# The order of work inside the chunk steps of a two-stack transformer kernel

## The chip, the cores and the metric

The kernel runs on one NeuronCore of a Trainium2 chip, in one launch. The metric is the device time of that core in microseconds (us). The engines are TensorE (PE, with its weight loads as PEld), VectorE (DVE), ScalarE (ACT), GpSimd (POOL) and SyncE (SP). All arithmetic is in float32.

## What is computed

The reference runs two stacks of two layers over a sequence of 512 rows of width 1024. Only the first stack is touched here. In it each layer holds a hybrid mixer (pooling, differential attention and a bidirectional RWKV-7 scan) and an MLP. The two parts that meet in the changed code are the attention and the scan, cut to what matters:

```python
def block(args):                       # attention, one block of 128 queries
    logits = jnp.einsum('bqhmd,bkhmd->bhmqk', q_blk, k) + bias
    p = jax.nn.softmax(logits, axis=-1)
    attn = p[:, :, 0] - lam * p[:, :, 1]
    return jnp.einsum('bhqk,bkhd->bqhd', attn, v)

def step(state, inp):                  # scan, per head, forwards and backwards
    sa = jnp.einsum('bhij,bhj->bhi', state, -kk_t)
    state = state * w_t + sa[..., None] * (kk_t * a_t) + v_t[..., None] * k_t
    return state, jnp.einsum('bhij,bhj->bhi', state, r_t)
```

## The kernel before, in words

The first stack has two layers, and each layer has four channel groups, so `group_pe`, `group_act` and `group_dve` run eight times. A group computes one attention head (two softmax maps `m`), and two RWKV heads in both directions `d`. After projections and the inversion of a triangular matrix per chunk (`level_w` to `corner_t`), the group goes through the **chunk steps**, the loop `for s in range(NCH)` at L892 with four steps of 128 rows. This text calls the four steps of one group a stage; there are eight stages in an execution. Every engine has its own program, and its order is written out by hand.

TensorE in a step, in the order of before:

- R products: per direction two 64-column products per head (L897), and from step 1 on the product with the state (L904), which waits for VectorE's state of the step before.
- The attention's value products of the block before (`heads_out(s - 1)`, L858, four products of 128x128 accumulated), from step 1 on.
- The attention's logits of the next block (`logits(s + 1)`, L851, two products of 64 rows by 512 columns), except in the last step.
- U products (L914), which need ScalarE's copies of R.
- State and output products (L923, L926, L928), then those that need ScalarE's copies of U (L932, L936).
- Four transposes of the block's probabilities (`turn`, L2096), after a wait for VectorE's `pnorm(s)`.

After the last step `heads_out(3)` follows. Each float32 product is recorded as two matmul instructions, so L897 counts x8 in a step; a transpose is one.

ScalarE copies PSUM tiles to SBUF in the order in which `gA` lists them (`take`, L958): R of both directions, the attention output `o`, U of both directions, the transposed probabilities `PT`. Then `probs(s + 1)` (L985) takes the two exponentials of the next block. VectorE does `pnorm(s)` (L1155 to L1160), `rowmax(s + 1)` (L1147, one reduction per map, out of the logits' PSUM tile), the state from the S tiles (L1221 to L1231), and the Y tiles (L1237, L1239).

PSUM tiles rotate through banks in the order of the two lists `gA` (banks 0 and 1, taken by ScalarE) and `gV` (banks 2 to 7, taken by VectorE). A tile can be opened once the tile two places (for `gA`) or six places (for `gV`) ahead in the list has been taken. R's two tiles are opened together, so R of the next step waits until ScalarE has copied the transposed probabilities. Within a step the U products wait for the copy of R of their direction (`took`, L911). No DMA is issued inside the steps.

Of the kernel before, what the change touches and what calls it, by code (L numbers as in the profile page):

```python
# [23 lines left out]
P = 128  # L24
D = 1024
S = 512
# [9 lines left out]
NCH = S // CHUNK  # L36
# [199 lines left out]
def build(nc, x_in, wts1, const1, onehot, rel_bias, meta, wts2, const2, out):  # L236
    ctx = ExitStack()
    with ctx:
# [337 lines left out]
        gV += [f"W{d}{h}_{HB}" for d in range(2) for h in range(2)] + ["l00", "l01"]  # L576
        gV += [f"T{d}{h}_{HB}" for d in range(2) for h in range(2)]
        for s in range(NCH):
            gA += [f"R{d}{s}" for d in range(2)] + [f"o{s - 1}"] * (s > 0) + [f"U{d}{s}" for d in range(2)] + [f"PT{s}"]
            if s < NCH - 1:  # L580
                gV += [f"l{s + 1}{m}" for m in range(2)] + [f"S{d}{s}" for d in range(2)]
            gV += [f"Y{d}{s}" for d in range(2)]
        gA += [f"o{NCH - 1}"]
        gA += ["yt", "oT"]
        grpA, grpV = Tiles(gA, BA), Tiles(gV, BV)
# [150 lines left out]
        def group_pe(pe, L, c, proj, proj_rows, slot, free, flush, turn, meet):  # L736
# [155 lines left out]
            for s in range(NCH):  # L892
                o = a.open_all([f"R{d}{s}" for d in range(2)])
                for d in range(2):
                    n = chunk[d][s]
                    for h in range(2):
                        m = pe.matmul(o[d][:, 64 * h:64 * h + 64], g2[d][h][:, n, 0, :], vN[:, n, 64 * h:64 * h + 64],  # L897
                                      start=h == 0, stop=s == 0, skip_group_check=True)
                    if s == 0:
                        a.close(m)  # L900
                if s:
                    for d in range(2):
                        took(pe, grpV, vb, v_taken, f"S{d}{s - 1}")
                        a.close(pe.matmul(o[d][:, 0:P], ar[d][:, chunk[d][s], 0, :], state[d], start=False, stop=True,  # L904
                                          skip_group_check=True))
                    heads_out(s - 1)
                if s < NCH - 1:
                    logits(s + 1)
                for d in range(2):
                    n = chunk[d][s]  # L910
                    took(pe, grpA, ab, a_taken, f"R{d}{s}")  # L911
                    o = a.open(f"U{d}{s}")
                    for h in range(2):
                        m = pe.matmul(o[:, 64 * h:64 * h + 64], TT[d][h][:, n, :], Rs[d][:, 64 * h:64 * h + 64],  # L914
                                      start=h == 0, stop=True, skip_group_check=True)
                    a.close(m)
                last = s == NCH - 1
                o = v.open_all([f"S{d}{s}" for d in range(2) if not last] + [f"Y{d}{s}" for d in range(2)])
                so, yo = o[:-2], o[-2:]
                for d in range(2):  # L920
                    n = chunk[d][s]
                    if not last:
                        pe.matmul(so[d][:, 0:P], kN[d][:, n, :], vN[:, n, :], start=True, stop=False, skip_group_check=True)  # L923
                    for h in range(2):
                        c_ = slice(64 * h, 64 * h + 64)
                        pe.matmul(yo[d][:, c_], g2[d][h][:, n, 1, :], vN[:, n, c_], start=h == 0, stop=False, skip_group_check=True)  # L926
                    if s:
                        pe.matmul(yo[d][:, 0:P], ar[d][:, n, 1, :], state[d], start=False, stop=False, skip_group_check=True)  # L928
                for d in range(2):
                    took(pe, grpA, ab, a_taken, f"U{d}{s}")  # L930
                    if not last:
                        v.close(pe.matmul(so[d][:, 0:P], bN[d][:, chunk[d][s], :], Us[d], start=False, stop=True, skip_group_check=True))  # L932
                for d in range(2):
                    for h in range(2):
                        c_ = slice(64 * h, 64 * h + 64)
                        m = pe.matmul(yo[d][:, c_], g1[d][h][:, chunk[d][s], 1, :], Us[d][:, c_], start=False, stop=True, skip_group_check=True)  # L936
                    v.close(m)
                pe.wait_ge(*at("pnorm", it, s))
                turn(a, f"PT{s}", [pr[s % 2][:, 0, b * P:(b + 1) * P] for b in range(4)])
            heads_out(NCH - 1)  # L940
# [7 lines left out]
        def group_act(act, L, c, meet):  # L948
            it = L * GROUPS + c
            ab, vb = a_grp(L, c), v_grp(L, c)  # L950
            a = Taker(act, grpA, ab, a_made, a_taken)

            def col(name):
                return gp[:, GC[name]:GC[name] + 1]

            def take(name, dst, f=ACT.Copy, n=S, **kw):
                o = a.open(name)
                a.close(act.activation(dst, o[:, 0:n], f, **kw))  # L958

            def flat(z):  # L960
                return z.rearrange("p a b -> p (a b)")

            act.dma_start(skew, skew_dram[bass.ds(c, 1), P - 1:P - 1 + P * (LINE - 1)]
                          .rearrange("o (p n) -> (o p) n", n=LINE - 1)[:, 0:SKEW]).then_inc(skew_loaded, 16)
            for i, n in enumerate(("zr", "zk", "zv")):
                take(n, zp[:, i, 1:S + 1])
            act.wait_ge(*at("params", it))
            for t, buf in (("w", sig), ("a", aa)):
                for d in range(2):
                    take(f"{t}{d}", buf[:, d, :], ACT.Sigmoid, bias=col(f"{t}0_{d}"))  # L970
            take("u", up_[:, 8:8 + S])
            act.wait_ge(*at("ssq_max", it))
            act.activation(sq, kk, ACT.Sqrt).then_inc(STEPS["nrm_root"][0], 1)

            def exps(d):
                act.wait_ge(*at("cums", it, d))
                act.activation(ep[d][:, 0, :], cumx[d], ACT.Exp, scale=-KAPPA)
                act.activation(ep[d][:, 1, :], cum[d], ACT.Exp, scale=-KAPPA)
                act.activation(en[d], cum[d], ACT.Exp, scale=KAPPA)
                act.activation(e0[:, d, :], mid[:, d, :], ACT.Exp, scale=-KAPPA).then_inc(STEPS["exps"][0], 1)  # L980

            def probs(i):
                for m in range(2):
                    act.wait_ge(*at("logit_max", it, 2 * i + m))
                    act.activation(pr[i % 2][:, m, :], pr[i % 2][:, m, :], ACT.Exp, scale=-1.0, bias=ast[:, 16 * (i % 2) + m:16 * (i % 2) + m + 1],  # L985
                                   accum_out=ast[:, 16 * (i % 2) + 2 + m:16 * (i % 2) + 3 + m]).then_inc(STEPS["probs"][0], 1)

            take("aq", aq, scale=64 ** -0.5)
            take("ak", ak)
            exps(0)  # L990
            take("av", flat(av))
            exps(1)
            take("gate", gate)
            take("vN", flat(vN))
            for d in range(2):
                take(f"bN{d}", flat(bN[d]))
                take(f"kN{d}", flat(kN[d]))
            o = a.open("pool")
            a.close(act.activation(flat(yT[:, bass.ds(c, 1), :]), o, ACT.Copy, scale=col("pscale")))
            probs(0)  # L1000
            for s in range(NCH):
                for d in range(2):
                    take(f"R{d}{s}", Rs[d], n=P)
                if s:
                    take(f"o{s - 1}", osb[:, s - 1, :], n=P)
                for d in range(2):
                    take(f"U{d}{s}", Us[d], n=P)
                take(f"PT{s}", flat(pT))
                if s < NCH - 1:
                    probs(s + 1)  # L1010
            take(f"o{NCH - 1}", osb[:, NCH - 1, :], n=P)
            act.wait_ge(*at("osub", it))
            act.activation(ast[:, 12:16], ast[:, 8:12], ACT.Sqrt).then_inc(STEPS["osqrt"][0], 1)
            act.wait_ge(*at("gn_var", it))
            act.activation(gns[:, 2, :], gns[:, 1, :], ACT.Sqrt).then_inc(STEPS["gn_root"][0], 1)
            take("yt", kt[0], ACT.Identity, scale=col("gng"), bias=col("gnb"))

            act.wait_ge(*at("onorm", it))
            take("oT", flat(yT[:, bass.ds(c + 4, 1), :]), scale=ast[:, 7:8])
            a.end()  # L1020
            meet(m_grp(L, c, 0))
# [9 lines left out]
        def group_dve(dve, L, c, meet):  # L1031
# [182 lines left out]
            for s in range(NCH):  # L1214
                pnorm(s)
                if s < NCH - 1:
                    rowmax(s + 1)
                    if s:
                        for d in range(2):
                            n = chunk[d][s]  # L1220
# [12 lines left out]
                for d in range(2):  # L1233
                    n = chunk[d][s]
                    o = v.open(f"Y{d}{s}")
                    if s < 2:
                        v.close(dve.tensor_copy(ysum[:, n, :], o[:, 0:P]))  # L1237
                    else:
                        v.close(tt(ysum[:, n, :], ysum[:, n, :], o[:, 0:P], ALU.add))  # L1239
                dve.drain()  # L1240

            took(dve, grpA, ab, a_taken, "o3")
# [1375 lines left out]
```

## Time and profile before

| | us |
|---|---|
| time, median of 3 runs | 4862.07 (4854.64 to 4862.35) |
| time of the profiled execution | 4859.53 |
| its span in the profile | 4857.8 |
| TensorE busy | 4502.2 (93% of the span) |
| VectorE busy | 1481.6 (30%) |
| ScalarE busy | 828.7 (17%) |
| mean granted TensorE clock | 0.953 of full speed |

The span is the time from the first to the last instruction that the profile shows; the execution's own time is 1.7 us longer. The granted clock is a share of 2.4 GHz: 1.00 is 2.4 GHz and 0.50 is 1.2 GHz. Matmul records are modelled at their ends, so the start times of the groups are what counts: the distance from the start of one group to the start of the next is what the group costs.

### The profile page before, as it was taken

Reading aid. Unit: us, or ns where it says so; the run is one execution under the profiler, and the core shown is the slowest. Engines: PE = TensorE matmul, PEld = TensorE weight load, DVE = VectorE, ACT = ScalarE, POOL = GpSimd, SP = SyncE. Lnnn points to the kernel's source line nnn. Section 1 sums busy time; section 2 is a strip of 40 time slices with the busy share of each in tenths; the row PEclk is TensorE's granted clock in tenths of the full one; section 3 lists DMA queues with packets and bytes.
Section 4 is the critical chain, followed back from the end, with each engine's and each line's share of the span. In section 5 each row is a group of like instructions: output and inputs, shape, how many; then the busy total and the mean of one; then the engine's idle time right before and its main releaser. Section 6 shows DMA issues by size and latency. Waiting matters only on the chain.

```text
span 4857.8 us, 60662 instructions
## 1 busy us (share of the span) xinstructions
PE 4502.2 (93%) x25140; PEld 2959.1 (61%) x25140; DVE 1481.6 (30%) x3621; ACT 828.7 (17%) x2097; POOL 146.4 (3%) x144
## 2 busy tenths in 40 slices
PE   7888898998999888888998999999999999999999
PEld 3755665443444466567443444477887788788888
DVE  2654662111000456546111000222122322212332
ACT  3112211001000211212101000122222212222220
POOL 0000000000000000000000000000110000001000
PEclk9898898999999988989999999999999999999999
DMA  3010011221222100100221222111111111111111
GB/s 107 15 40 31 10 40 35 87 83 57 74 77 75 56 18 23 39 22 19 76 87 57 74 78 74 56 57 44 53 48 48 53 61 57 48 53 53 53 53 66
DMA packets 71344, 261.62 MB, mean 54 GB/s; under 512 B 7920, under 2 KB 7920, under 8 KB 70816
## 3 DMA queue, kind: packets, MB, share of 16 engines
q1 hardware_dynamic: 69168, 250.62, 14.9%
q10 hardware_dynamic: 1904, 7.11, 0.4%
q8 instruction: 203, 3.33, 0.3%
q14 instruction: 69, 0.57, 0.0%
HBM read 253.51 MB, written 4.19 MB: 53 GB/s over the span
## 4 chain that ended last, share of the span: by engine, by line
PE 89%; DVE 5%; ACT 3%; DVEq 1%; issue 1%; DMA 0%; ACTq 0%; SPq 0%; PEldq 0%
PE ps L2075 27%; PE ps L1313 23%; PE ps L2186 9%; PE ps L1482 4%; PE ps L2152 3%; PE ps L1332 2%; PE ps L1416 2%; PE ps L2105 2%; PE ps L808 2%; PE ps L816 2%; PE ps L823 1%; PE ps L782 1%; PE ps L2086 1%; PE ps L2096 1%; ACT arena L958 1%
## 5 line engine op out<-in xcount | busy, mean ns | idle before, releaser
L2075 PE MATMUL ps<-xT,ring 128*128 128x512 f32 x2656 | 1185.6, 607 | 73.4 <-ACTq L661 47.1
L2075 PEld LDWEIGHTS ps<-xT,ring 128*128 128x128 f32 x2656 | 514.2, 195 | 738.2 <-issue 738.2
L1313 PE MATMUL ps<-xT,ring 128*128 128x264 f32 (+2 forms) x3392 | 795.3, 390 | 17.1 <-DVE arena L1802 10.4
L1313 PEld LDWEIGHTS ps<-xT,ring 128*128 128x128 f32 (+1 forms) x3392 | 640.2, 192 | 135.7 <-DVE arena L1802 13.9
L2186 PE MATMUL ps<-arena,ring 128*128 128x512 f32 x1024 | 440.4, 592 | 1.9 <-issue 1.9
L2186 PEld LDWEIGHTS ps<-arena,ring 128*128 128x128 f32 x1024 | 194.2, 190 | 248.1 <-issue 247.6
L1313 PE MATMUL ps<-arena,ring 128*128 128x264 f32 (+1 forms) x1408 | 320.3, 385 | 2.3 <-DVEq L1702 2.3
L1313 PEld LDWEIGHTS ps<-arena,ring 128*128 128x128 f32 x1408 | 265.9, 191 | 46.3 <-issue 6.1
L1572 ACT ACTIVATE arena<-ps 128x264 f32<-128x264 f32 (+8 forms) x316 | 122.7, 389 | 727.3 <-PE ps L1313 614.1
L958 ACT ACTIVATE arena<-ps 128x128 f32<-128x128 f32 (+1 forms) x296 | 122.8, 424 | 666.7 <-PE ps L2075 330.7
L2096 PE MATMUL ps<-consts,arena 128*128 128x128 f32 x384 | 72.7, 339 | 124.3 <-DVEq L1038 100.7
L2397 DVE TENSOR_TENSOR arena<-arena 128x512 f32<-128x512 f32 x64 | 44.3, 692 | 413.3 <-ACT arena L2290 413.3
L1908 DVE TENSOR_TENSOR arena<-ps,arena 128x128 f32<-128x128 f32 (+1 forms) x108 | 31.3, 290 | 451.0 <-PE ps L1482 451.0
L2152 PE MATMUL ps<-yT,ring 128*128 128x512 f32 x384 | 167.4, 592 | 0.0
L2404 DVE SCALAR_TENSOR_TENSOR xT<-xT,ps 128x512 f32<-128x512 f32 x16 | 11.0, 688 | 430.1 <-PE ps L2186 430.1
L2096 PEld LDWEIGHTS ps<-consts,arena 128*128 128x128 f32 x384 | 57.9, 182 | 136.2 <-DVEq L1038 105.4
L2227 ACT ACTIVATE arena<-xT 128x512 f32<-128x512 f32 x40 | 24.1, 630 | 625.1 <-DVE xT L2318 625.1
L2152 PEld LDWEIGHTS ps<-yT,ring 128*128 128x128 f32 x384 | 73.0, 190 | 91.8 <-issue 91.8
L2374 DVE TENSOR_TENSOR arena<-ps,arena 128x512 f32<-128x512 f32 x16 | 11.1, 692 | 371.4 <-PE ps L2152 371.4
L2075 PE MATMUL ps<-arena,ring 128*128 128x512 f32 x256 | 110.9, 594 | 5.0 <-DVEq L2381 3.5
L1916 DVE SCALAR_TENSOR_TENSOR arena<-ps,arena 128x128 f32<-128x128 f32 (+1 forms) x108 | 30.1, 279 | 275.6 <-PE ps L1452 273.5
L1482 PEld LDWEIGHTS ps<-arena 128*128 128x128 f32 (+2 forms) x736 | 95.2, 184 | 27.4 <-issue 17.6
(310 smaller groups left out, 4998.4 us busy)
## 6 DMA issues: line engine op xcount, KB each, us to landing
ring<-in_weights SPq DMA_DIRECT2D x467, 512.0 KB, 3.4
arena<-skew_dram ACTq DMA_DIRECT2D x8, 448.0 KB, 3.1
arena<-in_x SPq DMA_DIRECT2D x1, 2048.0 KB, 10.9
out_rows<-arena SPq DMA_DIRECT2D x8, 256.0 KB, 2.7
skew_dram<-arena ACTq DMA_DIRECT2D x4, 511.5 KB, 5.8
consts<-in_const SPq DMA_DIRECT2D x1, 1384.0 KB, 5.9
consts<-in_const ACTq DMA_DIRECT2D x1, 1252.0 KB, 5.6
arena<-in_buckets SPq DMA_DIRECT2D x1, 127.9 KB, 10.9
```

Source lines behind the costliest of these rows:

```text
L808: m = pe.matmul(o[h][r, k], g1[d][h][r, n, 0, r], X[d][h][r, n, :], start=True, stop=True)
L816: m = pe.matmul(o[h][r, k], XT[d][h][r, n, :], W[d][h][r, n, :], start=True, stop=True)
L958: a.close(act.activation(dst, o[:, 0:n], f, **kw))
L1313: mm = pe.matmul(o[0:m, 0:cols.stop - cols.start], ws[:, k, 0:m], src[:, k, cols], start=k == 0, stop=k == nk - 1)
L1332: mm = pe.matmul(o[0:n, t * P:(t + 1) * P], xT[:, k, k0:k0 + n], w[:, k, :], start=k == 0, stop=k == KD - 1)
L1416: mm = pe.matmul(ps[0:nq, SB + h, 0:main[0] + main[1] - lo], q, k[:, lo:main[0] + main[1]], start=True, stop=True)
L1482: mm = pe.matmul(ps[0:nq, OM, 64 * h:64 * h + 64], lh, rh, start=j == 0, stop=j == len(todo) - 1)
L1572: m = act.activation(dst, src, f, **kw)
L2075: m = pe.matmul(o, w[:, k, :], src[:, k, 0:S], start=k == 0, stop=k == KD - 1)
L2096: m = pe.transpose(o[:, n * P:(n + 1) * P], src4[n], ident)
L2152: m = pe.matmul(o, w[:, 4 * (n % 2) + k, :], yT[:, 4 * n + k, :], start=k == 0, stop=k == 3)
L2186: m = pe.matmul(o, w[:, k, :], hid[:, s * KD + k, :], start=s == 0 and k == 0, stop=s == 3 and k == KD - 1)
```

## The change

In each chunk step the U products follow the R products directly, on TensorE and in ScalarE's order of copies. The value products of the block before and the logits of the next block stand behind the output products, ahead of the transposes. VectorE's `rowmax(s + 1)` moves from behind `pnorm(s)` to the end of the step, behind the Y tiles. The lists of PSUM tiles are reordered in the same way, so tiles fall on other banks. No instruction is added or removed.

```diff
         for s in range(NCH):
-            gA += [f"R{d}{s}" for d in range(2)] + [f"o{s - 1}"] * (s > 0) + [f"U{d}{s}" for d in range(2)] + [f"PT{s}"]
+            gA += [f"R{d}{s}" for d in range(2)] + [f"U{d}{s}" for d in range(2)] + [f"o{s - 1}"] * (s > 0) + [f"PT{s}"]
             if s < NCH - 1:
-                gV += [f"l{s + 1}{m}" for m in range(2)] + [f"S{d}{s}" for d in range(2)]
-            gV += [f"Y{d}{s}" for d in range(2)]
+                gV += [f"S{d}{s}" for d in range(2)]
+            gV += [f"Y{d}{s}" for d in range(2)] + [f"l{s + 1}{m}" for m in range(2) if s < NCH - 1]
...
                         a.close(pe.matmul(o[d][:, 0:P], ar[d][:, chunk[d][s], 0, :], state[d], start=False, stop=True,
                                           skip_group_check=True))
-                    heads_out(s - 1)
-                if s < NCH - 1:
-                    logits(s + 1)
...
                     v.close(m)
+                if s:
+                    heads_out(s - 1)
+                if s < NCH - 1:
+                    logits(s + 1)
                 pe.wait_ge(*at("pnorm", it, s))
...
                 for d in range(2):
                     take(f"R{d}{s}", Rs[d], n=P)
+                for d in range(2):
+                    take(f"U{d}{s}", Us[d], n=P)
                 if s:
                     take(f"o{s - 1}", osb[:, s - 1, :], n=P)
-                for d in range(2):
-                    take(f"U{d}{s}", Us[d], n=P)
...
                 pnorm(s)
                 if s < NCH - 1:
-                    rowmax(s + 1)
...
+                if s < NCH - 1:
+                    rowmax(s + 1)
                 dve.drain()
```

## Rows read from the trace of the kernel before

**Rows 1.** The page: span, and the granted clock in 40 equal slices (tenths).

```profile
span 4857.8 us, 60662 instructions
...
PEclk9898898999999988989999999999999999999999
```

**Rows 2.** The page: the chain that ended last, shares of the span by engine.

```profile
PE 89%; DVE 5%; ACT 3%; DVEq 1%; issue 1%; DMA 0%; ACTq 0%; SPq 0%; PEldq 0%
```

**Rows 3.** Busy time by stage: start:end, length, PE, PEld, DVE, ACT, POOL, PEclk, DMA share, GB/s.

```profile
377.42:417.89 40.47, 37.16 (x228) 31.39 (x228) 16.53 (x52) 11.76 (x35) 0.00 (x0) 0.79 0.00 1
554.05:592.89 38.84, 35.53 (x228) 30.98 (x228) 16.53 (x52) 11.77 (x35) 0.00 (x0) 0.82 0.00 1
728.27:774.49 46.22, 43.11 (x229) 37.24 (x229) 16.61 (x52) 11.82 (x35) 0.00 (x0) 0.67 0.00 1
...
sum 329.03, PE 302.73 PEld 257.62 DVE 132.38 ACT 94.18 POOL 0.00; mean PE 37.84 PEld 32.20 DVE 16.55 ACT 11.77 POOL 0.00
```

**Rows 4.** Timeline of a full-rate step in the second stage: start, length, instructions [idle before].

```profile
401.15 1.10 PE L897 MATMUL ps<-arena 128*128 128x64 f32 x8 [0.69 <-ACT arena L958]
...
402.10 0.66 PE L904 MATMUL ps<-arena 128*128 128x128 f32 x4
...
402.57 0.50 ACT L958 ACTIVATE arena<-ps 128x128 f32<-128x128 f32 x2
...
402.99 1.13 PE L858 MATMUL ps<-arena 128*128 128x128 f32 x8 [0.23 <-ACT arena L958]
...
404.05 1.13 PE L851 MATMUL ps<-arena 64*128 64x512 f32 x4
...
405.21 0.69 DVE L1147 CUSTOM_DVE_ANT_0 arena<-ps,arena 128x512 f32<-128x512 f32 x1 [0.98 <-PE ps L851]
...
409.18 0.61 PE L2096 MATMUL ps<-consts,arena 128*128 128x128 f32 x4
...
409.82 0.60 ACT L958 ACTIVATE arena<-ps 128x512 f32<-128x512 f32 x1 [3.29 <-PE ps L2096]
...
410.47 1.10 PE L897 MATMUL ps<-arena 128*128 128x64 f32 x8 [0.69 <-ACT arena L958]
...
411.02 0.71 ACT L985 ACTIVATE arena<-arena 128x512 f32<-128x512 f32 x1
```

**Rows 5.** Timeline of step 0 in the second stage.

```profile
377.42 1.08 PE L897 MATMUL ps<-arena 128*128 128x64 f32 x8 [2.02 <-DVE arena L1212]
...
378.09 0.28 ACT L958 ACTIVATE arena<-ps 128x128 f32<-128x128 f32 x1 [1.55 <-PE ps L897]
...
378.43 2.08 PE L851 MATMUL ps<-arena 64*128 64x512 f32 x4
```

**Rows 6.** Timeline of step 1 in the fourth stage, all of it at half clock.

```profile
739.21 1.97 PE L897 MATMUL ps<-arena 128*128 128x64 f32 x8 [0.69 <-ACT arena L958]
...
742.18 2.05 PE L858 MATMUL ps<-arena 128*128 128x128 f32 x8
744.16 2.08 PE L851 MATMUL ps<-arena 64*128 64x512 f32 x4
746.16 1.97 PE L914 MATMUL ps<-arena 128*128 128x64 f32 x8
...
753.90 1.06 PE L2096 MATMUL ps<-consts,arena 128*128 128x128 f32 x4
755.65 1.97 PE L897 MATMUL ps<-arena 128*128 128x64 f32 x8 [0.69 <-ACT arena L958]
```

**Rows 7.** Busy time and granted clock in parts of the second, third and fourth stage.

```profile
379.42:392.42 13.00, 12.28 (x54) 10.60 (x51) 4.59 (x14) 3.11 (x9) 0.00 (x0) 0.50 0.01 1
392.42:397.42 5.00, 5.00 (x27) 3.49 (x26) 1.35 (x4) 0.83 (x3) 0.00 (x0) 0.69 0.00 0
...
569.05:574.05 5.00, 5.00 (x37) 4.09 (x37) 1.93 (x7) 0.83 (x3) 0.00 (x0) 0.95 0.00 0
...
748.27:761.27 13.00, 12.28 (x56) 11.06 (x55) 3.38 (x11) 3.01 (x9) 0.00 (x0) 0.52 0.00 0
```

## The prediction

> **What bounds the kernel now.** I read the page first. TensorE's clock strip is near full, with dips in the first half only, where the first stack runs [rows 1], and the chain that ended last is 89% TensorE [rows 2]. So a change of order counts if TensorE idles less or runs at another clock. Then I summed the eight stages that the change touches, each from its first R product to the start of the last value products: 329.03 us, 6.8% of the span. VectorE is busy 16.53 of 40.47 us in one of them and ScalarE 11.76, so neither bounds them. TensorE is busy 37.16 of 40.47, and that is much the same work at every stage, yet the stages last from 38.84 to 46.22 us, and the length goes with the mean granted clock, 0.82 down to 0.67 [rows 3]. The clock is therefore the second thing to price, beside the waits.
>
> The third view is the timeline of one step at full clock, 401.15 to 410.47, that is 9.32 us from R to R. It holds two stalls. The R products wait until ScalarE has copied the transposed probabilities: transposes start at 409.18, R at 410.47, 1.29 us for about 0.5 us of work, so some 0.8 us idle. The value products wait until R of direction 0 is copied: L904 starts at 402.10, the value products at 402.99, some 0.35 us idle [rows 4]. The same step at half clock takes 755.65 - 739.21 = 16.44 us [rows 6].
>
> The fourth view is the clock by stretch. In the second stage it stands at 0.50 from 379.42 to 392.42 and averages 0.69 over the next 5 us, so it rose at 392.42 + 5.00 - (0.19 / 0.5) x 5.00 = about 395.5, 18.1 us into the stage. What TensorE did just before was the value products and the logits of step 1 one after the other. In the fourth stage it did not rise there; it averages 0.52 in 748.27 to 761.27, so it rose near 760.7, 32.5 us in, in the same group of step 2 [rows 7]. The third stage, read in the same way, rose 15.5 us in [rows 7]; the other five, whose windows repeat the pattern of the second, rose 18 to 20 us in, in the same group of step 1.
>
> **The change, part by part.** No instruction comes or goes and no DMA moves: SP's and POOL's queues carry nothing in the steps.
>
> *U right behind R, steps 1 to 3.* Before, the value products were the ones that stood waiting for the copy of R0; after, U stands there, for the same copy. The stall of 0.35 us stays (ScalarE starts both R copies in 0.50 us at 402.57, so direction 1 is ready before U of direction 0 has run [rows 4]). Gain 0. That is the point of the change, and the trace shows nothing for it to recover: the copies of U were hidden by the output products before, and still are.
>
> *U right behind R, step 0.* Before, nothing waited: logits at 378.43, 1.01 us after R. After, U waits for a copy that starts 0.67 us in [rows 5] and wakes TensorE 0.42 us after its start (402.57 to 402.99 [rows 4]): 1.09 us. Cost 0.08 us, taken as 0.1 a stage, 0.8 us in all. If direction 1 is late too it is at most 0.4 a stage, 3 us.
>
> *Logits and rowmax at the end of the step.* What could be late next is ScalarE: the exponentials now hang on a later rowmax, and the next R copies queue behind them. At full clock, from the start of the logits: rowmax starts 1.16 us in and takes 0.69 (405.21 - 404.05); the second follows, about 2.8. The transposes come 1.06 in, their copy 0.64 later, done at 2.30, the first exponential (0.71) at 3.0. So both maxima are there when ScalarE comes to them. The exponentials end near 3.8, and the next R0 is finished at about 1.06 + 1.29 + 0.95 + 0.47 = 3.8 [rows 4]. No wait, but no margin: I take 0, and keep 0.2 us x 24 steps = 5 us for the range. The VectorE work `pnorm(s + 1)` then waits for the exponentials ahead of the state; the state is wanted a whole step later, and VectorE is idle for more than half of the stage [rows 3], so 0. A gain is excluded from the state's earlier finish: in no stage does R wait for VectorE's state. The banks turn in another order, but every tile is taken long before its successor opens: 0.
>
> *The transposes' wait* (0.8 us) is the same before and after: the value products that could have covered it now stand in front of it, not behind it. Gain 0. Waits alone therefore sum to +0.8 us.
>
> *The clock.* In before, step 1 has L904, value products and logits in one run: 740.98 to 746.16 at half clock, 5.2 us [rows 6], of which L904 is the 1.2 us ahead of 742.18. The rises came in that run in seven stages of eight in step 1. After, the U products (64 columns, as R's) stand between L904 and the rest. Step 0 then has logits and transposes only, 2.0 + 1.06 us, starting near 8.2 us into the stage. Step 1 begins near 11.7, and if it stays at half clock, it lasts 16.44 us again. Its value products, logits and transposes start 16.44 - 1.98 - 2.00 - 1.75 = 10.7 us into it [rows 6], so they run from 22.4 to 27.5. I put the rise about 4 us into that run, 26.5 us in, where it was 18.1. A microsecond at half clock does 9.32 / 16.44 = 0.57 us of full-clock work, so it loses 0.43. Later by 8.4 us costs 3.6 us a stage. Where step 0's run of 3.1 us is enough, the rise comes near 11.5, 6.6 us earlier, and gains 2.8 us. Seven rises out of eight in a 5.2 us run say that a run that long mostly does it; one miss says that where it falls matters. The 3.1 us run is shorter, so I give it two stages of eight: 6 x 3.6 - 2 x 2.8 + 0.8 = **+16.8 us**. Ends: all eight early, -22 + 0.8; all eight late, +29, plus the 5 us above.
>
> A rule speaks to this. From 379.42 to 392.42 TensorE is busy 12.28 of 13.00 us, and the granted clock stays at 0.50, 1.2 GHz [rows 7]. The Trainium skill, "TensorE: Matmul & The Clock Gate", section "Part 1: The HAM clock gate", says that the throttled clock is the default and that sustained busy time of the array releases it. Taken as busy time in the records, it would make both orders alike and the change worth +0.8 us; the row disagrees with that reading, since a stretch that is busy nearly throughout did not release it, and the sum goes by the rows.
>
> **To the median.** The profiled execution took 4859.53 us for a span of 4857.8; 16.8 more is 4876.3. It lies 2.5 us under the median of 4862.07, and three runs spread over 7.7 us, so I forecast from the median: about 4878.
>
> **Rivals.** *The clock doesn't care about the order* (nothing but waits): 4862.07 + 0.8 = 4863. For it: the work per step is the same, and stages differ among themselves anyway. Against: seven of eight rises in one and the same group of instructions.
>
> *Step 0's run is enough nearly everywhere*, faster: the rise moves to 11.5 us in, 8 x -2.8 + 0.8 = -22, 4840 us. Its place is the logits and transposes of step 0, which before stood 8 us apart. It decides if five or more stages of eight rise there (5 x -2.8 + 3 x 3.6 is about -3; from six on it is clearly faster). For it: they are now adjacent. Against: the run is 3.1 us, and a longer one missed once.
>
> *The clock falls again.* After, a full-clock step has the two stalls (0.8 and 0.35 us) with only R, L904 and U between and behind them, where before the value products and logits came behind the second. If the clock falls there, the next step costs up to 16.44 - 9.32 = 7.1 us more. Four such falls give +28 on top, about 4905. No stage of before shows one.
>
> *Forecast.* Chances: forecast 0.55, indifferent clock 0.22, early rise 0.13, falls 0.10. The stages may mix, which smears all of these. The range of 8 in 10 goes from 4848 to 4898. A measurement of this kernel tells about 0.2% (9.7 us) from no change. Faster by more than that takes most of the early-rise case: 0.13. Within: the indifferent clock and mixtures close to it, 0.24. Slower: 0.63.
>
> **What would show it.** In the profile after: the stages' sum (329.03 before) is longer by the change in time, and everything outside is about equal. U follows R's L904 by 0.9 us at full clock. The idle time before R stays at 0.69, by ScalarE's copy. The rise stands behind step 1's logits, near 26 us, in most stages, and mean clocks of the stages are 0.65 to 0.70. It is wrong if the rises stay near 18 us, if ScalarE's exponentials hold the R copies up (a longer distance from L904 to U), or if clock changes outside the stages outweigh those inside.

## The result, and the profile after

| | before | changed |
|---|---|---|
| median of 22 runs each, us | 4857.39 (4849.59 to 4862.35) | 4864.22 (4856.32 to 4867.07) |
| profiled execution, its span | 4857.8 | 4854.5 |
| mean granted clock in it | 0.953 | 0.953 |

The ratio is 1.0014, with a 95% interval of 1.0007 to 1.0020: the changed kernel is slower by 0.14%, 6.8 us by the medians. The forecast was 16.8 us slower, so the direction held and the size did not. The profiled execution is the fastest of the changed kernel's 22, and its span is even 3.3 us under that of before, so each kernel was profiled a second time, and both profiles are used. One execution of an experiment (4977.35 us at a mean granted clock of 0.914, its neighbours at 4813 to 4824 us) is 3% slower than the rest of its kernel and is left out of every comparison.

The page of the first profile of the changed kernel, span and granted clock in 40 slices, which answer to [rows 1]:

```profile
span 4854.5 us, 60662 instructions
...
PEclk9898899999999979989999999999999999999999
```

Five of the eight stages of the same profile, start:end, length, busy times, PEclk (this is the view of [rows 3], whose sum was 329.03):

```profile
202.57:243.02 40.45, 37.20 (x229) 32.01 (x229) 16.62 (x52) 11.76 (x35) 0.00 (x0) 0.79 0.00 1
377.60:415.22 37.62, 34.16 (x228) 29.08 (x228) 16.52 (x52) 11.71 (x35) 0.00 (x0) 0.86 0.00 1
551.11:594.81 43.70, 40.45 (x228) 34.48 (x229) 16.63 (x52) 11.75 (x35) 0.00 (x0) 0.73 0.00 1
729.23:766.90 37.67, 34.22 (x228) 29.13 (x228) 16.52 (x52) 11.71 (x35) 0.00 (x0) 0.86 0.00 1
1737.98:1786.06 48.08, 44.84 (x229) 39.06 (x229) 16.61 (x52) 11.76 (x35) 0.00 (x0) 0.65 0.00 1
...
sum 326.55, PE 299.72 PEld 256.42 DVE 132.55 ACT 93.84 POOL 0.00; mean PE 37.47 PEld 32.05 DVE 16.57 ACT 11.73 POOL 0.00
```

The stages fall into kinds. Four of them take 37.6 to 37.7 us, less than any stage of before, two take 43.7, one 48.1, and the first 40.45. VectorE's and ScalarE's busy times are the same in all of them. The length goes with the clock, 0.86, 0.73 and 0.65. The clock by stretch, in the second stage (two lines), the fifth (two) and the third (two):

```profile
379.60:389.60 10.00, 9.31 (x39) 7.29 (x39) 3.12 (x10) 1.44 (x4) 0.00 (x0) 0.53 0.01 2
389.60:410.00 20.40, 18.32 (x142) 15.61 (x141) 10.41 (x35) 8.28 (x26) 0.00 (x0) 1.00 0.00 1
1764.00:1773.00 9.00, 8.08 (x64) 6.78 (x60) 4.97 (x16) 3.06 (x9) 0.00 (x0) 0.96 0.01 3
1773.00:1786.06 13.06, 11.45 (x64) 9.89 (x62) 3.45 (x10) 4.21 (x12) 0.00 (x0) 0.74 0.00 0
553.11:574.11 21.00, 20.28 (x87) 18.00 (x87) 6.79 (x22) 3.42 (x11) 0.00 (x0) 0.50 0.00 1
574.11:580.11 6.00, 5.08 (x26) 3.02 (x25) 1.71 (x7) 2.70 (x8) 0.00 (x0) 0.78 0.00 0
```

In the second stage the clock is back at full by 389.1, 11.4 us in, right behind the logits and transposes of step 0. In the third it rises at 574.11 + 6.00 - (0.28 / 0.5) x 6.00 = 576.8, 25.7 us in. In the fifth it rose at 1773.00 - (0.96 - 0.50) / 0.5 x 9.00 = 1764.7, 26.7 us in, and fell again inside the last step: a mean of 0.74 up to the stage's end.

The timeline of the second stage, step 0 and the start of steps 1 and 2, answers to [rows 4, 5]; L911 are the U products, L2098 the transposes, L959 ScalarE's copies:

```profile
377.60 1.08 PE L897 MATMUL ps<-arena 128*128 128x64 f32 x8 [2.02 <-DVE arena L1213]
...
378.27 0.28 ACT L959 ACTIVATE arena<-ps 128x128 f32<-128x128 f32 x1 [1.55 <-PE ps L897]
...
378.69 1.82 PE L911 MATMUL ps<-arena 128*128 128x64 f32 x8
...
385.55 2.08 PE L851 MATMUL ps<-arena 64*128 64x512 f32 x4
...
387.56 1.11 PE L2098 MATMUL ps<-consts,arena 128*128 128x128 f32 x4
...
389.36 1.10 PE L897 MATMUL ps<-arena 128*128 128x64 f32 x8 [0.69 <-ACT arena L959]
...
390.30 0.66 PE L904 MATMUL ps<-arena 128*128 128x128 f32 x4
...
391.20 1.07 PE L911 MATMUL ps<-arena 128*128 128x64 f32 x8 [0.23 <-ACT arena L959]
...
398.69 1.10 PE L897 MATMUL ps<-arena 128*128 128x64 f32 x8 [0.69 <-ACT arena L959]
```

U starts 1.09 us after R in step 0, and 0.90 us after L904 in step 1, as the value products did. A full-clock step is 398.69 - 389.36 = 9.33 us, against 9.32. These distances came out as forecast; what step 0 and the last step cost at full clock is seen further down.

### The profile page after: what moved, and what is told of

It reads as the page before. It is cut to its first block, busy times and chain, and to the rows that moved or that the text cites. A ratio compares the mean times of both kernels' runs of the same rounds, so it can differ in the third digit from the quotient of the medians.

```text
span 4854.5 us, 60662 instructions
## 1 busy us (share of the span) xinstructions
PE 4499.4 (93%) x25140; PEld 2957.2 (61%) x25140; DVE 1482.1 (31%) x3621; ACT 827.8 (17%) x2097; POOL 146.3 (3%) x144
## 4 chain that ended last, share of the span: by engine, by line
PE 89%; DVE 5%; ACT 3%; DVEq 1%; issue 1%; DMA 0%; ACTq 0%; SPq 0%; PEldq 0%
PE ps L2077 27%; PE ps L1315 23%; PE ps L2188 9%; PE ps L1484 4%; PE ps L2154 3%; PE ps L1334 2%; PE ps L1418 2%; PE ps L2107 2%; PE ps L808 2%; PE ps L816 2%; PE ps L823 1%; PE ps L782 1%; PE ps L2098 1%; PE ps L2088 1%; ACT arena L959 1%
## 5 line engine op out<-in xcount | busy, mean ns | idle before, releaser
L1315 PEld LDWEIGHTS ps<-xT,ring 128*128 128x128 f32 (+1 forms) x3392 | 640.0, 192 | 135.7 <-DVE arena L1804 13.9
L959 ACT ACTIVATE arena<-ps 128x128 f32<-128x128 f32 (+1 forms) x296 | 122.6, 424 | 663.5 <-PE ps L2077 328.9
L2098 PE MATMUL ps<-consts,arena 128*128 128x128 f32 x384 | 74.9, 346 | 124.4 <-DVEq L1039 100.7
L2098 PEld LDWEIGHTS ps<-consts,arena 128*128 128x128 f32 x384 | 56.5, 177 | 162.5 <-DVEq L1039 105.4
```

Of the source, the lines that this page charges most:

```text
L1315: mm = pe.matmul(o[0:m, 0:cols.stop - cols.start], ws[:, k, 0:m], src[:, k, cols], start=k == 0, stop=k == nk - 1)
L2098: m = pe.transpose(o[:, n * P:(n + 1) * P], src4[n], ident)
```

## The experiments

Only the edit of each kernel is shown. Ratios are to runs of before that were measured beside the experiment: 4859.79 us beside the two halves of the change and the two runs with six extra products, 4853.09 us beside the two kernels that have four extra products ahead of step 0 and no other edit, and beside the last version, and 4860.51 us beside all others.

**Each half of the change alone.** The first edit moves only the logits and `rowmax`:

```diff
-                if s < NCH - 1:
-                    logits(s + 1)
                 for d in range(2):
                     n = chunk[d][s]
                     took(pe, grpA, ab, a_taken, f"R{d}{s}")
...
+                if s < NCH - 1:
+                    logits(s + 1)
                 pe.wait_ge(*at("pnorm", it, s))
```

> Half of the change: only the logits, their maxima and their tiles move to the end of the step; the value products stay between R and U. Clock theory (the order matters through the point at which the granted clock rises): in step 0 the logits and transposes stand side by side and can lift the clock near 11.5 us into the stage, while step 1 keeps L904 and the value products side by side ahead of U; so at least half of the eight stages rise near 11.5 us and none later than step 1 ends, and the time is 5 to 20 us below before. Wait theory (the order matters through which work hides ScalarE's copies): nothing waits more than in before but step 0's U, 0.1 us a stage, so the time is before plus 1 us, and the stages' rises stay near 18 us.

Measured: 4868.33 us, ratio 1.0021 (1.0012 to 1.0030), span 4868.7. Both theories missed: by the ratio it is slower by 10 us. In its profile the stages sum to 341.35 us; six of them rise 22.1 to 22.2 us in, the other two 22.7 and 23.2. Here is where, in the second stage, as timeline and as clock of the stretch 400.12 to 404.12:

```profile
401.13 0.95 PE L924 MATMUL ps<-arena 128*128 128x64 f32 x4
401.88 0.74 PE L926 MATMUL ps<-arena 128*128 128x128 f32 x2
402.41 1.03 PE L930 MATMUL ps<-arena 128*128 128x128 f32 x4
403.26 1.01 PE L934 MATMUL ps<-arena 128*128 128x64 f32 x8
```

```profile
400.12:404.12 4.00, 4.00 (x24) 4.00 (x23) 0.98 (x4) 0.00 (x0) 0.00 (x0) 0.61 0.00 0
```

The clock rose at 404.12 - (0.11 / 0.5) x 4.00 = 403.2, behind state and output products, with no value products or logits running. So "the rise comes behind the run of values and logits" describes most stages and does not hold always: step 0's logits and transposes did not lift the clock in any stage of this profile, though the same pair did in four of the changed kernel's. The full-clock step is longer here, 9.52 us (406.61 to 416.13), against 9.32 in before.

The second edit moves only the value products and their copy behind the output products (TensorE, ScalarE and `gA`, as in the change), and leaves the logits between R and U.

> The other half: only the value products and their copy move to the end of the step; the logits stay between R and U. Clock theory: step 0 is that of before, and step 1 has L904 and logits, then value products and transposes, as two runs of about 3 us in place of one of 5.2; some stages rise only in step 2, 25 to 33 us in, and the time is 10 to 30 us above before. Wait theory: the logits need no copy of R and so hide it again; the stall of 0.35 us ahead of the value products goes in steps 1 and 2 of every stage, and the time is 4 to 6 us below before.

Measured: 4865.99 us (single executions from 4848.06 to 4876.21), ratio 1.0016 (1.0006 to 1.0027). By the ratio it is slower by 8 us, just under the clock theory's range; its stages sum to 337.9 us, six rising 25 to 26 us in, at the end of step 1. The wait theory was right on the wait, for a full-clock step takes 417.08 - 408.18 = 8.90 us, since the logits hide the copy of R (they start 0.60 us behind L904, where the value products of before start 0.89 behind it). The clock took that gain back and more.

```profile
408.18 1.10 PE L897 MATMUL ps<-arena 128*128 128x64 f32 x8 [0.69 <-ACT arena L959]
409.12 0.66 PE L904 MATMUL ps<-arena 128*128 128x128 f32 x4
409.72 1.13 PE L851 MATMUL ps<-arena 64*128 64x512 f32 x4
...
417.08 1.10 PE L897 MATMUL ps<-arena 128*128 128x64 f32 x8 [0.69 <-ACT arena L959]
```

**Holding the clock up.** TensorE idles 2.02 us ahead of step 0 [rows 5]. Products whose result nobody reads fill it (six in the first two runs, four later, since six ended after the wait):

```diff
             for d in range(2):
                 corner_t(d)
+            spare = a.open_all([f"R{d}0" for d in range(2)])[0][:, 256:512]
+            for _ in range(6):
+                pe.matmul(spare, ones, ak[:, 0:256], start=True, stop=True, skip_group_check=True)
             for d in range(2):
                 took(pe, grpV, vb, v_taken, f"T{d}1_{HB}")
```

> Before, with six extra products (128x128 by 256 columns, result never read) in TensorE's idle time of 2 us ahead of step 0. Clock theory: the clock no longer falls at the start of the stage, every stage takes 33 to 34 us in place of 38.8 to 46.2, and the time is 50 to 65 us below before. Wait theory: work put into idle time changes nothing, within 2 us of before.

Measured: 4803.0 us, ratio 0.9887 (0.9874 to 0.9900), 57 us faster. All eight stages take 32.97 us, with no half-clock time in them.

> The same six products in the changed kernel. Clock theory: the two orders now differ by step 0's 0.1 us a stage alone, 0 to 2 us over the kernel before with the same products, unless the clock falls inside a step (R, L904 and U with two stalls and no value products or logits between), which costs up to 7 us each time and shows as stages over 40 us. Wait theory: the changed kernel's own time, within 2 us.

Measured: 4818.38 us (the median of four executions), ratio 0.9919 (0.9904 to 0.9933). Neither the 0 to 2 us nor the kernel's own time: 15.4 us over the other order. Its profile is of the execution that is left out, so it can't tell why; further runs below ask whether it is the clock falling inside a step.

**The changed kernel once more, and before once more.**

> The changed kernel as it is, looked at once more. Clock theory: the points at which the clock rises in the eight stages (11.4 us into the stage in four, 19 to 27 in the others, in the first look) fall otherwise, the sum of the stages differs from 326.55 us by several us, and the difference of the two spans is that of the stages' sums within 3 us. Wait theory: the stages last the same to 1 us each.

Measured: 4864.61 us, span 4862.8, near the median of the 22 runs. Its stages:

```profile
203.69:251.53 47.84, 44.59 (x228) 39.10 (x228) 16.69 (x52) 11.75 (x35) 0.00 (x0) 0.65 0.00 1
...
sum 334.04, PE 307.18 PEld 263.58 DVE 132.57 ACT 93.83 POOL 0.00; mean PE 38.40 PEld 32.95 DVE 16.57 ACT 11.73 POOL 0.00
```

The spans of the two profiles differ by 8.3 us and the stages' sums by 7.5. Nearly all of it is the first stage, 47.84 in place of 40.45: its clock rose 26 us in, and fell again in the last step. The other seven stages are within 0.1 us of the first profile. One kernel, two executions, and the clock's course alone between them. I call the second of them the typical execution.

> The kernel before, looked at once more. Clock theory: seven or eight of the eight stages rise 15 to 20 us in, each of these takes 38.8 to 41.7 us, and a stage that does not rise there takes about 46; the sum is 323 to 331 us. Wait theory: all stages as in the first look.

Measured: 4860.06 us, span 4858.3, sum of stages 329.01, each stage as in the first profile within 0.02 us. The fourth takes 46.21 again. Both theories allowed this, so it decides nothing between them. No profile shows one of the executions of before at 4850 to 4853 us.

**Does the clock fall inside a step?** Warm start in the changed kernel, with and without one more product in the idle time behind the transposes:

```diff
                 turn(a, f"PT{s}", [pr[s % 2][:, 0, b * P:(b + 1) * P] for b in range(4)])
+                if not last:
+                    took(pe, grpV, vb, v_taken, f"S1{s}")
+                    for _ in range(1):
+                        pe.matmul(so[1][:, 256:512], ones, ak[:, 0:256], start=True, stop=True, skip_group_check=True)
```

> The changed kernel with four extra products in the idle time ahead of step 0 (six before, which ended after the wait they were to fill), and one more (128x128 by 256 columns) in the idle time behind the transposes of steps 0 to 2. Clock theory: with the extra product between transposes and R the clock does not fall inside a step, all eight stages take 33.2 to 33.6 us, and the time is 4796 to 4806. If instead the excess of the changed kernel with warm start over before with warm start (15 us) is waiting, it stays: 4810 to 4818.

Measured: 4792.42 us (4790.08 to 4793.84), ratio 0.9864 (0.9847 to 0.9881), a little below the range of the clock theory. All eight stages take 33.04 us at full clock.

> The changed kernel with four extra products ahead of step 0 and none inside the steps. Clock theory: the clock does not fall at the stage's start but can fall inside a step, so it lies 10 to 25 us over the same kernel with the extra product behind the transposes (4792.4): 4802 to 4817, and its profile shows stages of 33.2 us and stages of 37 us or more, the long ones with a half-clock stretch inside. Wait theory: no difference to that kernel, 4790 to 4794.

Measured: 4814.96 us, ratio 0.9916 (0.9901 to 0.9931). One stage takes 33.04 us and seven take 36.3. Two stages of it, and two stretches of the second of them:

```profile
374.49:407.53 33.04, 29.58 (x228) 25.45 (x229) 16.43 (x52) 11.71 (x35) 0.00 (x0) 1.00 0.00 1
542.26:578.56 36.30, 32.84 (x228) 28.72 (x228) 16.43 (x52) 11.72 (x35) 0.00 (x0) 0.91 0.00 1
565.00:572.00 7.00, 6.08 (x40) 4.80 (x40) 3.36 (x10) 3.33 (x10) 0.00 (x0) 0.91 0.00 0
572.00:578.00 6.00, 5.88 (x28) 5.64 (x28) 0.57 (x2) 0.36 (x2) 0.00 (x0) 0.54 0.00 0
```

The timeline around the fall, at 572.00 - (0.09 / 0.5) x 7.00 = 570.7:

```profile
568.09 1.10 PE L900 MATMUL ps<-arena 128*128 128x64 f32 x8 [0.69 <-ACT arena L962]
569.03 0.66 PE L907 MATMUL ps<-arena 128*128 128x128 f32 x4
569.93 1.21 PE L914 MATMUL ps<-arena 128*128 128x64 f32 x8 [0.23 <-ACT arena L962]
570.93 1.06 PE L926 MATMUL ps<-arena 128*128 128x64 f32 x4
```

It stands right behind R, the state's product (L907 here) and U (L914 here) with the two stalls, as the rival "the clock falls again" placed it. The other six falls stand 2.5 to 2.8 us into a step as well, five of them in step 3 and one, the first stage's, in step 2. Seven falls at 36.30 - 33.04 = 3.26 us make 22.8 us; the two kernels differ by 22.5. One product in each of the three gaps of a stage, which shortens the idle time ahead of R from 0.69 to 0.25 us, takes all of it away.

**What the waits alone are worth.**

> The kernel before with four extra products in place of six. With the clock held up at all times, only waits differ between the orders: the stages take 32.97 us as with six, against 33.04 in the changed order, and the time lies within 2 us of the changed kernel with warm start and the extra product (4792.4), 4790 to 4794. If the orders differed by their waits as the 6.8 us between the kernels ask, it would lie near 4786.

Measured: 4791.77 us (4789.97 to 4792.35), ratio 0.9868 (0.9853 to 0.9883), stages 33.04 to 33.05 us (not 32.97, which is the length behind six products). The second stage of this kernel, and of the changed one with the extra product in the gaps:

```profile
371.18:404.23 33.05, 29.53 (x228) 25.40 (x229) 16.43 (x52) 11.71 (x35) 0.00 (x0) 1.00 0.00 1
```

```profile
371.28:404.32 33.04, 30.88 (x234) 26.26 (x234) 16.42 (x52) 11.72 (x35) 0.00 (x0) 1.00 0.00 1
```

The starts of R in steps 0, 1 and 3 of the same two stages:

```profile
371.18 1.08 PE L900 MATMUL ps<-arena 128*128 128x64 f32 x8
...
378.16 1.10 PE L900 MATMUL ps<-arena 128*128 128x64 f32 x8 [0.69 <-ACT arena L961]
...
396.81 1.10 PE L900 MATMUL ps<-arena 128*128 128x64 f32 x8 [0.69 <-ACT arena L961]
```

```profile
371.28 1.07 PE L900 MATMUL ps<-arena 128*128 128x64 f32 x8
...
378.46 1.10 PE L900 MATMUL ps<-arena 128*128 128x64 f32 x8 [0.25 <-ACT arena L966]
...
397.10 1.10 PE L900 MATMUL ps<-arena 128*128 128x64 f32 x8 [0.25 <-ACT arena L966]
```

Step 0 takes 7.18 us in the changed order and 6.98 in the old one, 0.20 more. The last step takes 404.32 - 397.10 = 7.22 against 404.23 - 396.81 = 7.42, 0.20 less. So with the clock up the waits of the two orders cancel, and the stages sum to 264.34 and 264.36 us. The medians differ by 0.65 us, but the executions of the two kernels overlap, so neither the prediction's 0.8 nor zero is excluded by the times. Either way most of the 6.8 us is not waiting.

**The same product without the warm start.**

> The changed kernel with one extra product in the idle time behind the transposes of steps 0 to 2, and no warm start, so that the clock falls at the start of the stage as always. Clock theory: logits, transposes and the extra product of step 0 make a run of 3.5 us and lift the clock near 11.5 us into the stage in six stages or more; those take 37.6 to 38.0 us, and the time is 4820 to 4850, below both kernels. Wait theory: idle time filled changes nothing, 4864 within 4 us.

Measured: 4839.01 us, ratio 0.9961 (0.9948 to 0.9974), faster than both kernels. Seven of eight stages are back at full clock 11.3 to 13.0 us in and take 37.5 to 38.6 us, the first takes 40.46, and they sum to 304.3 against 334.0 in the typical execution.

**A version that beats both.** Value products late, logits between R and U, and four products ahead of step 0:

> Only the value products late, logits between R and U, and the four extra products ahead of step 0. With the clock held up the order is left with its waits alone: a full-clock step took 8.90 us in this order against 9.32 in before's, so two steps of eight stages give 7 us below before with six extra products (4803.0), and two fewer extra products give up to 5 more: 4788 to 4798. If the shorter step is given back elsewhere, it is 4798 to 4803.

Measured: 4788.92 us (4788.61 to 4789.38), ratio 0.9858 (0.9843 to 0.9873). The stages take 32.00 us. Half of the change is a gain of 2.9 us over the old order (4791.77) once the clock is out of it. I expected 7 from the steps. The stages gave that, 1.05 us each and 8.4 in all, but some 5 us are lost again outside them. They are lost between the stages: from the end of the second to the start of the third it is 135.14 us, against 134.71 in the old order with four products, and from the fifth to the sixth 136.41 against 134.16. Why is open.

The same with sixteen products of 512 columns ahead of the closing transposes:

> The order with only the value products late, four extra products ahead of step 0, and sixteen more (128x128 by 512 columns) in the idle time of 8.6 us ahead of the transposes that close a group. Clock theory: the half-clock stretch of 13.7 us behind each stage goes, 2 to 3.5 us a group are saved, and the time is 4760 to 4774, against 4788.9 without the sixteen. If the closing part is bound by VectorE and the weights' loads alone, it is 4786 to 4792.

Measured: 4815.91 us, ratio 0.9918 (0.9901 to 0.9935), 27 us slower than without. The timeline of the closing part behind the second stage, without the sixteen products (first) and with them (second):

```profile
402.89 1.16 PE L858 MATMUL ps<-arena 128*128 128x128 f32 x8 [0.69 <-ACT arena L962]
412.64 1.97 PE L2100 MATMUL ps<-consts,arena 128*128 128x128 f32 x8 [8.59 <-DVEq L1042]
```

```profile
406.47 13.90 PE L946 MATMUL ps<-arena,consts 128*128 128x512 f32 x32
420.21 1.04 PE L2102 MATMUL ps<-consts,arena 128*128 128x128 f32 x8
```

The clock did stay up (mean 0.978 over the span, 0.968 without), but the products took 13.9 us where 8.6 were free. I had sized them by the logits, 1.06 us for two products, and they cost 0.87 each. The closing transposes come 5 us later behind the stage than without; the next stage starts only 3.6 us later (138.76 us behind the end of this one against 135.14), with a mean clock of 0.96 against 0.91 in that stretch, so the clock gave something back. The size was wrong; the idea is not refuted, nor shown.

## Why the prediction was right or wrong

*U right behind R gains nothing, the waits sum to +0.8 us.* Right in the main: the stall of L904 to the next products is 0.90 us in both orders, and with the clock held up the stages of the two orders are equally long. The two parts are off: step 0 costs 0.20 us, not 0.1, and the last step, which the sum left at 0, gives 0.20 back.

*Logits and rowmax late cost nothing.* Right: the step is 9.33 us, ScalarE was in time.

*The clock prices the change.* Right, and shown from both sides: the times of the two orders are 0.65 us apart with the clock held up and 6.8 us without, and the course of the clock accounts for the difference of two executions of one kernel.

*"I give it two stages of eight"*: this is the term that failed. In both profiles four stages rose behind step 0's logits and transposes. Three of them gain the 2.8 us that was forecast, where before rose in step 1 (40.47 to 37.7). The fourth stage gains 8.5, since in before it was the one that had missed step 1 (46.22); the sum took it at the usual 18 us.

*6 x 3.6 for a rise at 26.5.* The late rises stand at 25.7 to 26.7, so place and price were near: the third stage lost 4.9 and the seventh 3.2. Only these two are plain cases.

*The rival "the clock falls again"*, given 0.10 and kept out of the sum, happened as well: twice in the typical execution, in the first and the fifth stage. Their last step takes 10.48 us, in place of the 7.22 of a stage without such a fall, so a fall cost 3.26 us, under half of the "up to 7.1". With the late rise, these two stages lost 6.2 and 7.6 us. The typical sum is then -8.5 - 3 x 2.8 + 4.9 + 3.2 + 6.2 + 7.6 = +5.0 us, by the two profiles 334.04 - 329.01 = 5.0. The spans differ by 4.5, the medians by 6.8. What is missing up to 6.8 is that the profiled execution of before lies 2.7 us above its median; no profile shows one of its faster executions.

Forecast and rivals, told as alternatives, were present in one execution together. And the direction was right by luck: the two falls, which the sum had at nothing, make 6.5 us, more than the whole 5.0. Without them the early and late rises come to -1.5 us, for the gains of four stages then outweigh the losses of the other four, and the sum's own terms, at their measured numbers and sizes, say that nothing changes.

The prediction also reads its rows too neatly where it puts seven rises of before "in that run" of value products and logits. The windows of the first, sixth and eighth stage put theirs up to 0.7 us behind it, in the U products (sixth stage: full clock from 1938.3, U starts at 1937.69). And 4862.07 + 16.8 is 4878.9, where the prediction writes about 4878.

The rule of the Trainium skill ("TensorE: Matmul & The Clock Gate", "Part 1: The HAM clock gate"), read as busy time in the records, fails here as it did before: from 553.11 to 574.11 TensorE is busy 20.28 of 21.00 us at 0.50.

*What decides in a given stage.* The prediction did not ask why the stages of before differ, and counted early stages by the length of a run. The stages do not start alike: the clock falls from full to half at the stage's start, and not always at the same point. The first 2 us of four stages of the changed kernel's first profile (the first, second, third and fifth), and of the first stage of the second profile:

```profile
202.57:204.57 2.00, 1.99 (x17) 1.88 (x17) 1.41 (x4) 0.81 (x3) 0.00 (x0) 1.00 0.00 0
377.60:379.60 2.00, 1.99 (x13) 1.88 (x14) 1.41 (x4) 0.55 (x2) 0.00 (x0) 0.81 0.00 0
551.11:553.11 2.00, 1.99 (x16) 1.88 (x16) 1.41 (x4) 0.80 (x3) 0.00 (x0) 0.95 0.00 0
1737.98:1739.98 2.00, 2.00 (x10) 2.00 (x10) 1.40 (x4) 0.31 (x2) 0.00 (x0) 0.50 0.00 0
```

```profile
203.69:205.69 2.00, 2.00 (x10) 2.00 (x10) 1.41 (x4) 0.30 (x2) 0.00 (x0) 0.50 0.00 0
```

A mean of 0.81 over 2.00 us puts the fall 1.2 us in, 0.95 puts it 1.8 us in, 1.00 behind the 2 us, and 0.50 ahead of the stage. In both profiles every stage that fell about 1.2 us in (mean 0.78 to 0.81) rose 11.4 to 11.5 us in, every one that fell about 1.8 us in (0.94 to 0.97) rose 25.7 to 25.8 us in, the one that fell behind the 2 us rose 19.2 us in, and the three that fell ahead of the stage rose 26.2 to 26.7 us in and fell again. The first stage, in which the two executions part, differs from its very first product: R takes 1.08 us in one and 1.94 in the other. In before a mean of 0.94 goes with the rise at 32.5 us and 0.97 with the one at 15.5, so little more than 0.1 us in the fall goes with 7.4 us of stage (46.22 against 38.84). This is read from profiles; no run set the point of the fall on purpose.

*Open:* what places the fall, and why a given order turns it into an early or a late rise. The fall alone does not tell: in the second experiment the sixth and the seventh stage have the same mean of 0.81 over their first 2 us, and one rises 25.1 and the other 21.7 us in.

## What to carry to other kernels

When a reordering removes no work, hold the clock up in both orders (one cheap product in each idle gap) and measure again: only then do the waits show, and here they were 0.65 of 6.8 us. The larger prize was the clock itself, 1.3% or about 64 us for four unread products ahead of each stage. Size such filler by a product of its own shape: six products in place of four cost about 10 us here (4803.0 against 4791.77), and the sixteen that outlasted their gap cost 27. And profile a kernel more than once before a difference of a few us is explained from one profile.

## What the runs showed that I had not expected

- One kernel has distinct courses of the clock from execution to execution: the same first stage took 40.45 and 47.84 us, and a single profile had the sign of the change the wrong way round (its span 3.3 us shorter, the median 6.8 us longer).
- At full clock, a product of 128 rows by 512 columns took 0.87 us (13.90 / 16), one of 64 rows by 512 columns 0.53 (1.06 / 2).
- The clock fell 5.7 us into a stretch of 7.00 us in which TensorE was busy 6.08, with single gaps of 0.69 and 0.23 us, and with one product of 256 columns in each larger gap it fell in none of the eight stages.
